# Sparse-attention and SwiGLU block on one core: the output projection of the last group with 512 moving columns, weights streamed twice

## What is computed

```python
def nsa_mixer(h, ...):                       # 16 heads in 4 groups, head width 128
    proj = h @ w_in
    ...
    def block(qb):                           # compressed, selected and window branch
        ...
        return gx[..., 0:1] * o_cmp + gx[..., 1:2] * o_sel + gx[..., 2:3] * o_win
    out = ...                                # S x (16 heads * 128)
    return out @ w_out                       # 512x2048 @ 2048x2048

x = x + nsa_mixer(rms_norm(x, norm_mix_g), ...)
h = rms_norm(x, norm_ffn_g)
x = x + (silu(h @ wg) * (h @ wu)) @ wd
```

## Time and profile before

| | |
|---|---|
| median of 3 runs | 2169.27 us (2169.15 to 2170.48) |
| profiled execution, its own time | 2169.41 us |
| its span, first to last instruction | 2167.6 us |
| mean granted TensorE clock | 1.000 |
| PE busy | 2156.6 us (99% of the span) |
| PE weight loads (PEld) busy | 1850.3 us (85%) |
| DVE busy | 1550.5 us (72%) |
| ACT busy | 1036.9 us (48%) |
| POOL busy | 103.9 us (5%) |
| moved by DMA | 301.94 MB |

### The profile page before, as it was taken

One profiled execution on the slowest core, in us unless ns is written; L12 is line 12 of the kernel. 1 busy time (PEld: TensorE's weight loads), 2 busy tenths in 40 slices (PEclk: granted clock), 3 DMA queues, 4 the chain that ended last, 5 costly groups with the idle time before them and its releaser, 6 DMA issues.

```text
span 2167.6 us, 29862 instructions
## 1 busy us (share of the span) xinstructions
PE 2156.6 (99%) x11261; PEld 1850.3 (85%) x11261; DVE 1550.5 (72%) x2230; ACT 1036.9 (48%) x1481; POOL 103.9 (5%) x123
## 2 busy tenths in 40 slices
PE   9999999999999999999999999999999999999999
PEld 8898988989889998788888888888888888888887
DVE  6333566675676554897777777777777898989898
ACT  5332344443453344854445445444544565555553
POOL 1001000000000000000000000000000000000000
PEclk9999999999999999999999999999999999999999
DMA  5444232232224223655555455465555677666655
GB/s 179 116 111 99 82 68 60 69 69 59 53 75 147 78 69 107 199 157 174 141 156 188 113 171 174 129 176 164 161 157 162 199 211 234 185 199 194 180 143 163
DMA packets 209871, 301.94 MB, mean 139 GB/s; under 512 B 18924, under 2 KB 116497, under 8 KB 208321
## 3 DMA queue, kind: packets, MB, share of 16 engines
q1 hardware_dynamic: 197618, 254.74, 37.4%
q0 software_dynamic: 12112, 45.31, 9.9%
HBM read 236.79 MB, written 28.59 MB: 122 GB/s over the span
## 4 chain that ended last, share of the span: by engine, by line
PE 96%; DVE 2%; ACT 1%; issue 1%; DMA 0%; POOL 0%; SPq 0%; DVEq 0%; ACTq 0%
PE ps L1736 93%; PE ps L2048 1%; PE ps L2118 1%; DVE wl L1088 1%; ACT wh L674 0%; DMA x_rows<-in_x_dram 0%; DVE x_rows L1121 0%; ACT left_val L934 0%; DVE hTl L1088 0%; PE ps L2028 0%; PE ps L2083 0%; DVE ptl L1409 0%; ACT sq L969 0%; DVE pbuf L1386 0%; ACT pbuf L834 0%
## 5 line engine op out<-in xcount | busy, mean ns | idle before, releaser
L674 ACT ACTIVATE wh<-g 128x1024 fp32r<-128x1024 f32 x462 | 490.1, 1062 | 580.4 <-PE ps L1736 444.0
L1088 DVE TENSOR_TENSOR wl<-g,wh 128x1024 fp32r<-128x1024 f32 x462 | 565.1, 1224 | 227.3 <-PE ps L1736 219.6
L1736 PE MATMUL ps<-wh,left_hi 128*128 128x512 f32 x1232 | 481.9, 391 | 0.9 <-DVE wl L1088 0.5
L1736 PE MATMUL ps<-wh,left_lo 128*128 128x512 f32 x1232 | 479.7, 389 | 0.0
L1736 PE MATMUL ps<-wl,left_hi 128*128 128x512 f32 x1232 | 479.4, 389 | 0.0
L1736 PEld LDWEIGHTS ps<-wh,left_hi 128*128 128x128 f32 x1232 | 231.3, 188 | 50.4 <-issue 2.6
L1736 PEld LDWEIGHTS ps<-wh,left_lo 128*128 128x128 f32 x1232 | 231.2, 188 | 48.4
L1736 PEld LDWEIGHTS ps<-wl,left_hi 128*128 128x128 f32 x1232 | 231.3, 188 | 47.2
L1736 PE MATMUL ps<-wh,down_hi 128*128 128x512 f32 x616 | 239.8, 389 | 0.0
L1736 PE MATMUL ps<-wh,down_lo 128*128 128x512 f32 x616 | 239.7, 389 | 0.0
L1736 PE MATMUL ps<-wl,down_hi 128*128 128x512 f32 x616 | 239.6, 389 | 0.0
(11 more groups left out here) (212 smaller groups left out, 3027.9 us busy)
## 6 DMA issues: line engine op xcount, KB each, us to landing
g<-in_ffn_w_gate_dram SPq DMA_DIRECT2D x176, 256.0 KB, 3.2
g<-in_ffn_w_up_dram SPq DMA_DIRECT2D x176, 256.0 KB, 4.2
g<-in_ffn_w_down_dram SPq DMA_DIRECT2D x176, 256.0 KB, 5.1
raw<-in_nsa_w_in_dram SPq DMA_DIRECT2D x152, 256.0 KB, 3.1
g<-g POOLq DMA_DIRECT2D x66, 512.0 KB, 5.0
down_val<-m_scratch SPq DMA_DIRECT2D x77, 256.0 KB, 4.8
raw<-in_nsa_w_out_dram SPq DMA_DIRECT2D x64, 256.0 KB, 3.1
m_scratch<-work SPq DMA_DIRECT2D x22, 384.0 KB, 2.9
```

The costliest lines, as they stand in the source:

```text
L674: return nc.scalar.activation(dst, src, ACT.Copy)
L1088: nc.vector.tensor_tensor(dst, src, hi.bitcast(f32), ALU.subtract).then_inc(done, 1)
L1736: return nc.tensor.matmul(out_, a, b, start=start, stop=stop, skip_group_check=True)
```

## The change

The 24 units of the last group become 48 (`OUT_K` = 6 per block of work, `B0 = A0 + 8 * OUT_K`), each of two k tiles by 512 columns. Block c = w // 6 is now a column block of 512 (c // 2) for one half of the tokens (c % 2), so the same weights are loaded and split for c = 2b and again for c = 2b + 1. `filler(w)` uses the whole of unit `A0 + w`: 12 matmuls of 512 moving columns, two token tiles, one in bank 6 and one in bank 7. The tables `HEAD_FILL`, `FILL_A`, `TAIL_A`, `END_A` are unchanged, and `after(j)` in the last group now lists every filler of the step instead of every second. Ahead of the loop four units are split, units 4 to 7: unit 4 between the two `first_out`, unit 5 after the first exponential (on VectorE the first maximum), units 6 and 7 after the compressed exponential (on VectorE after `compressed_scores`); the two splits that stood in iteration 1 are gone from there.

```diff
-B0 = A0 + 24
+OUT_K = 6
+B0 = A0 + 8 * OUT_K
...
             for c in range(8):
-                for q in range(3):
-                    n = A0 + 3 * c + q
-                    unit(n, k_halves(n, w_out_v[q][:, :, c * 256:(c + 1) * 256], 4))
+                for q in range(OUT_K):
+                    n = A0 + OUT_K * c + q
+                    unit(n, k_halves(n, w_out_v[q // 2][:, q % 2 * 2:q % 2 * 2 + 2, c // 2 * 512:(c // 2 + 1) * 512], 2))
...
                 def after(j):
-                    return ended(fill[j]) if last else late(fill, j)
+                    return fill[j] if last else late(fill, j)
...
                 if last:
-                    for q in range(4, OWN // 2):
-                        first_out(q)
+                    first_out(4)
+                    splits([0])
+                    first_out(5)
                 probs(0)
+                if last:
+                    splits([1])
                 compressed_exp()
+                if last:
+                    splits([2, 3])
                 for i in range(1, STEPS + 1):
                     if i < STEPS:
                         probs(i)
-                    if i == 1:
+                    if i == 1 and not last:
                         splits(ended(HEAD_FILL))
...
                 maximum(0)
+                if last:
+                    splits([1])
                 compressed_scores()
+                if last:
+                    splits([2, 3])
                 for i in range(1, STEPS + 2):
...
-                                at, src = x2[:, 2 * b:2 * b + 2, c * 256:(c + 1) * 256], (vst if c % 2 else kst)[:, b, :]
+                                at, src = x2[:, c % 2 * 2 + b, c // 2 * 512:(c // 2 + 1) * 512], (vst if c % 2 else kst)[:, b, :]
...
-                    c, q = u // 3, u % 3
-                    if half == 0 and 0 in tiles:
-                        arrive(A0 + u)
+                    c, q, n = w // OUT_K, w % OUT_K, A0 + w
+                    if 0 in tiles:
+                        arrive(n)
                         if c == 0:
-                            pe.wait_ge(ot_lo, 2 * q + 2)
-                    if q == 0 and c:
-                        pe.wait_ge(x2_staged, 2 * (c - 1) + half + 1)
-                    tokens_half(A0 + u, q, half, 6 + half, 12, tiles)
+                            pe.wait_ge(ot_lo, q + 1)
+                    for tt in tiles:
+                        if w == 0:
+                            wait(pe, q_lo, 3 + tt, 4, g)
+                        if q == 0 and c:
+                            pe.wait_ge(x2_staged, 2 * (c - 1) + tt + 1)
+                        ts = slice((c % 2 * 2 + tt) * P, (c % 2 * 2 + tt + 1) * P)
+                        for kk in range(2):
+                            k, at = 2 * q + kk, slice(kk * 512, kk * 512 + 512)
+                            last = mm3(bank(6 + tt), (hTh[:, k, ts], hTl[:, k, ts]), (wh[:, n % RING, at], wl[:, n % RING, at]),
+                                       k == 0, k == OWN - 1)
+                    if tiles[-1]:
+                        last.then_inc(units_used, 1)
```

More of the change, by code:

```diff
@@ L875, in splits @@
                     for u in units:
-                        if last and u % 3 == 2:
+                        if last and u % OUT_K == OUT_K - 1:
                             for half in range(2 - staged, 2):
@@ L899, in attention @@
                         for u in after(j):
-                            if u % 3 == 2:
+                            if u % OUT_K == OUT_K - 1:
                                 stage(u, 0)
@@ L917, in attention @@
                 head_out(REP - 1)
-                splits(ended(tail + [END_A] if last else tail), 2)
+                splits(tail + [END_A] if last else ended(tail), 2)
                 if not last:
@@ L1305, in after @@
                 def after(j):
-                    return ended(fill[j]) if last else late(fill, j)
+                    return fill[j] if last else late(fill, j)
                 def staged_added(units):
                     for u in units:
-                        if u % 3 == 2:
-                            if u == 2:
+                        if u % OUT_K == OUT_K - 1:
+                            if u == OUT_K - 1:
                                 dve.wait_ge(x2_loaded, 16 * TT)
-                            c = u // 3
+                            c = u // OUT_K
                             for b in range(2):
                                 dve.wait_ge(x2_staged, 2 * c + b + 1)
-                                at, src = x2[:, 2 * b:2 * b + 2, c * 256:(c + 1) * 256], (vst if c % 2 else kst)[:, b, :]
-                                nc.vector.tensor_tensor(at, at, src.rearrange("p (t c) -> p t c", t=2), ALU.add)\
-                                    .then_inc(x2a_added, 1)
+                                at, src = x2[:, c % 2 * 2 + b, c // 2 * 512:(c // 2 + 1) * 512], (vst if c % 2 else kst)[:, b, :]
+                                nc.vector.tensor_tensor(at, at, src, ALU.add).then_inc(x2a_added, 1)
                 def splits(units):
@@ L1426, in attention @@
                         compressed_weigh()
-                        splits(ended(HEAD_FILL))
+                        if not last:
+                            splits(ended(HEAD_FILL))
                     if i % 8 == 7 and i < STEPS - 1:
@@ L1465, in attention @@
                     staged_added(after(STEPS - 1))
-                    staged_added(ended(tail + [END_A]))
-                splits(ended(tail + [END_A] if last else tail))
+                    staged_added(tail + [END_A])
+                splits(tail + [END_A] if last else ended(tail))
             for g in range(LAST):
```

8 lines of the change are left out of this document (4 added, 4 removed).

## The result

The changed kernel takes 2177.66 us in the median of six runs (2176.66 to 2180.41) against 2169.36 before in the same job, a ratio of 1.0039 (95% interval 1.0029 to 1.0049). It is slower by 8.3 us, where 1.85 us less were forecast; the time lies above the range. The profiled execution took 2176.66 us with a span of 2174.9 (before: 2167.6).

The account below looks back on a forecast made before the run. TensorE's own work plus its waits was taken to bound the kernel: 7.2 us gained by width less 5.35 us of waits, net 1.85, gives 2167.5 us from 2169.27, range 2163.3 to 2171.5.

Parts of the forecast that it names:

- What bounds the kernel: Whole kernel: TensorE, busy 2156.6 of 2167.6 us; time is its own work plus the few places where it waits.
- The gain: Last group's 48 pieces: 12 matmuls of 512 columns for 24 of 256 save 0.15 us each, 7.2 us.
- Steps 10 and 18: Last group's loop, at ScalarE's copy of a finished head: second splits make TensorE wait 0.8 us, twice.
- Steps 22 and 27: Last group's loop, lone pieces with little cover: one more split per engine, 1.1 us more wait in each.
- stays hidden: Last group's added weight loads, 3.1 us median, 4.7 at most: covered, since the split comes a 6 us step later.
- Head: Before the last group's first compressed transposes: splits 6 and 7 ahead of VectorE's first weighing make TensorE wait 1.55 us.
- rival 3: Thin places open: seven column block changes 0.2 to 0.5 us each, head loads up to 1.6; 2169 to 2172.6; chance 0.12.
- Sum: Last group: waits of 5.35 us against 7.2 us gained, net 1.85 us gained.
- my case: Whole kernel: the forecast of 2167.5 us with its five waits, own range 2165.5 to 2170.5, chance 0.67.
- the second banks: Rival 3's part at seven column block changes: second bank's eviction late by up to 0.5 us; main forecast: cover 0.3 us.
- 2: Rival: added splits pace the loop, each that reaches TensorE costs 1.14 us; typically 15 places, 2179 us; chance 0.07.

Follow-up runs that it names:

- width_only: Kernel before with only the width changed, 12 matmuls of 512 columns per half unit for 24 of 256, loads and splits as before: 2163.25 us, ratio 0.9972.
- own_late: Changed kernel with VectorE's low half of a finished head taken one step later, where no split stands: 2175.53 us, ratio 1.0030.
- reload_late: Changed kernel with tiles 0 and 1 of `x` reloaded in the group before, tiles 2 and 3 only behind unit 7: 2173.25 us, ratio 1.0016.
- clock_kept: Changed kernel with 44 identity transposes into an unread bank ahead of the last group's first compressed transposes: 2175.13 us, ratio 1.0026.
- all_three: Changed kernel with `x` reload moved, VectorE's low half of finished heads a step later, and pieces 36 to 45 redistributed over steps: 2165.49 us, ratio 0.9984.
- late67: Changed kernel with splits 6 and 7 back in iteration 1, reload of `x` untouched: 2173.11 us, ratio 1.0018.
- rows_2k: Changed kernel with each tile of `x` reloaded by four requests of 2 KB rows in place of one of 8 KB: 2178.40 us, ratio 1.0040.

## Why the prediction was wrong

- **What bounds the kernel**: right. TensorE's own work plus its waits give the time, but TensorE's own work was priced at one clock throughout.
- **The gain**: 7.2 us forecast, 6.7 measured. The term was 0.15 us per piece and measured 0.14. By the formula in the Trainium skill, TensorE: Matmul & The Clock Gate, section "Back-to-back issue gap", it would have been 1.4 us, an estimate. The page gives it for an isolated matmul, not for a stream, which the prediction left out; the 6.2 us of width_only show that it does not price this stream.
- **Steps 10 and 18**: 0.8 us each forecast, 0.67 shown. Right, and by the named mechanism (own_late).
- **Steps 22 and 27**: 1.1 us more each forecast, 2.1 and 1.7 more measured. The sentence that failed here is that a load "stays hidden". It takes 3.6 us in the median now instead of 3.1, and a unit is loaded only when the split two before it is done. Where two splits stand in one step, the second waits for its own load. In step 22 ScalarE's two high halves start 2.24 us apart instead of 0.95; 0.6 of this is the eviction `vst` between them, which stood ahead of the single split before, and 0.69 is the load. With 0.20 ahead of the first it makes 0.9 us, nearly all of the 1.0 that the wait is over the forecast. The 0.95 us that I added for one more split left the load out.
- **Head**: this is the step that failed: "Splits 6 and 7 ... Wait 1.55 us". 5.55 us were shown. reload_late gives 1.40 at the same place, so the order was priced rightly and the loads wrongly. I had the cause as rival 3, with "up to 1.6 us" and 0.12, from the peak rate of the earlier trace rows. Four tiles of `x` and two units are 5.2 MB; they moved from 653.5 to 669.7 us, 323 GB/s on average and not 434. I also let the Trainium skill, DMA: Bandwidth & Descriptors, section "Queues, rings and completion order", count against that rival. It says that turns are taken packet by packet; that this gives a unit half of the rate was my inference, and it took the packets of both queues for equally large. The trace agrees with the turns, 327 packets of each queue in 8 us, but their bytes are 4 to 1. At a fifth of the 376 GB/s of that stretch, the 1.05 MB of units 6 and 7, one behind the other in SP's queue, would take 14 us, an estimate; the reload's last row at 668.5 us cut this short, and unit 7 landed at 669.7.
- **The clock**: not in the sum at all. About 2.5 us (clock_kept). The forecast head wait would hardly have brought it: behind the 1.40 us of reload_late and all_three the clock stays at 1.00.
- **Sum**: from before to after the waits shown grow by 5.55 us in the head, 1.34 in steps 10 and 18, 2.12 in step 22, 1.69 in step 27 and 0.1 elsewhere, together 10.8; with 2.5 for the clock and 6.7 of gain that is 6.6 of the 7.3 us of shift. The rest is about what the idle times leave out. They are counted from the recorded end of the last matmul, 0.39 us behind its start, where the next one would start after 0.23: at the five waits, 0.16 us each.
- **Rivals**: the half of 3 that lay in the head came, with 4.0 us above my case where it had up to 1.6, and the clock on top. Its other half, the second banks, did not: TensorE shows no wait at a change of column block in the changed kernel. 2 gave nearly the right time (2179) for a wrong reason: five places wait, not fifteen. The range failed because it took rival 3's upper bound from a peak rate and had no term for what a long gap does afterwards.

## What to carry to other kernels

Where a change takes away the slack of a load, price the load by all the bytes that must land before it, at the mean rate of the stretch and not the peak, and give the case that it lands last. Where streaming twice puts two splits in one step, the second waits for its own load: count the load in the chain. Price a long wait of TensorE with the clock that falls behind it, too. Repairs in one group are not separate: three small ones gave 12.2 us together and 8.8 apart, and only then the wider matmul paid (2165.5 us). When two queues share the DMA engines, compare the bytes per packet that the trace shows, not the rows that the request asks for.

## What was not expected of the hardware

- A wait of 5.55 us of TensorE costs about 2.5 us more in what follows, at a granted clock of 0.50; identity transposes in the gap remove that cost. Shorter waits can bring the fall too: it came behind 2.32 us (late67), 2.31 (clock_kept) and 1.84 (own_late), and not behind 2.12 and 2.08 in the changed kernel's trace or 1.40 in reload_late and all_three.
- A 512 KB unit (2 KB rows) loaded while POOL's queue reloads 4 MB in 8 KB rows gets a fifth of the bytes, packet for packet the same number, and lands over 10 us after issue, against 3.6 in the median. During a 2 MB reload it took 8.7 us, two of the last three with the DMA engines nearly idle; why stays open.
- A reload that asked for rows of 2 KB moved in packets of 4 KB (rows_2k).
